# A macaron decoder layer with a two-part fp32 product: inputs moved by a few bytes in SBUF, the first three units and the first norm in finer pieces, four small loads moved apart

## What is computed

```python
for l in range(DEPTH):                                   # DEPTH = 1
    x = x + 0.5 * swiglu(rms_norm(x, norm_ffn1[l]), ffn1_gate[l], ffn1_up[l], ffn1_down[l])
    h = rms_norm(x, norm_mix[l])
    proj = h @ w_in[l]                                   # 1024 x 5120
    qa, ka, va, rb, kb, vb, ga, gb = jnp.split(proj, splits, axis=-1)
    y_a = moba_attention(to_heads(qa), to_heads(ka), to_heads(va), rel_bias)
    y_b = rwkv7_time_mix(h, rb, kb, vb, mix_rkv[l], mix_wag[l], w_lora_a[l], w_lora_b[l], ...)
    merged = jax.nn.sigmoid(ga) * (y_a @ proj_a[l]) + jax.nn.sigmoid(gb) * (y_b @ proj_b[l])
    x = x + merged @ w_out[l]
    x = x + 0.5 * swiglu(rms_norm(x, norm_ffn2[l]), ffn2_gate[l], ffn2_up[l], ffn2_down[l])
return rms_norm(x, norm_final)

def swiglu(h, w_gate, w_up, w_down):
    return (jax.nn.silu(h @ w_gate) * (h @ w_up)) @ w_down   # 1024 -> 2816 -> 1024
```

## Time and profile before

| | us |
|---|---|
| median of 3 runs | 646.39 |
| the profiled execution | 644.8 |
| its span (first to last instruction) | 643.0 |
| PE busy | 630.7 (98%), 6738 matmuls |
| PEld busy | 615.9 (96%) |
| DVE busy | 423.1 (66%) |
| ACT busy | 295.5 (46%) |
| DMA | 105.38 MB, 164 GB/s in the mean |

### The profile page before, as it was taken

One profiled execution on the slowest core, in us unless ns is written; L12 is line 12 of the kernel. 1 busy time (PEld: TensorE's weight loads), 2 busy tenths in 40 slices (PEclk: granted clock), 3 DMA queues, 4 the chain that ended last, 5 costly groups with the idle time before them and its releaser, 6 DMA issues.

```text
span 643.0 us, 15489 instructions
## 1 busy us (share of the span) xinstructions
PE 630.7 (98%) x6738; PEld 615.9 (96%) x6738; DVE 423.1 (66%) x491; ACT 295.5 (46%) x343; POOL 90.6 (14%) x91
## 2 busy tenths in 40 slices
PE   8899999999999999999999999999999999999996
PEld 8899999999999999999988999999999999999996
DVE  4766688665556369968994437877766566665662
ACT  5734554343434274334665544545543444443341
POOL 0026800000113000020005533006000000000120
PEclk9999999999999999999999999999999999999999
DMA  9667655555556335583332232355655566545541
GB/s 309 193 199 226 197 170 177 183 180 180 180 179 196 103 132 176 179 189 125 123 105 96 68 102 71 128 172 191 189 169 175 186 196 195 185 154 199 170 143 65
DMA packets 100608, 105.38 MB, mean 164 GB/s; under 512 B 2196, under 2 KB 98684, under 8 KB 100564
## 3 DMA queue, kind: packets, MB, share of 16 engines
q1 hardware_dynamic: 99348, 101.45, 48.9%
q0 software_dynamic: 1056, 3.02, 2.1%
q10 hardware_dynamic: 160, 0.27, 0.1%
HBM read 103.48 MB, written 1.25 MB: 163 GB/s over the span
## 4 chain that ended last, share of the span: by engine, by line
PE 88%; DVE 5%; DMA 3%; ACT 2%; issue 0%; SPq 0%; DVEq 0%; ACTq 0%
PE two L1426 26%; PE two L1428 24%; PE two L1427 24%; PE two L1422 10%; DVE w_lo L885 2%; DMA w_raw<-in_ffn_gate 1%; ACT w_hi L521 1%; DMA w_raw<-in_ffn_up 1%; DMA x_tok<-in_x 1%; PE two L1691 1%; DVE hlo_f L904 1%; PE two L1693 1%; PE two L1692 1%; PE two L1834 0%; DVE w_lo L895 0%
## 5 line engine op out<-in xcount | busy, mean ns | idle before, releaser
L521 ACT ACTIVATE w_hi<-w_raw 128x2048 fp32r<-128x2048 f32 (+1 forms) x87 | 164.2, 1887 | 257.7 <-PE two L1428 231.7
L885 DVE TENSOR_TENSOR w_lo<-w_raw,w_hi 128x2048 fp32r<-128x2048 f32 (+1 forms) x87 | 202.5, 2327 | 89.4 <-ACT w_hi L521 89.1
L1426 PE MATMUL two<-hlo_f,w_hi 128*128 128x256 f32 x656 | 185.0, 282 | 2.7 <-DVE w_lo L885 1.5
L1427 PE MATMUL two<-hhi_f,w_lo 128*128 128x256 f32 x656 | 184.6, 281 | 0.0
L1428 PE MATMUL two<-hhi_f,w_hi 128*128 128x256 f32 x656 | 184.6, 281 | 0.0
L1426 PEld LDWEIGHTS two<-hlo_f,w_hi 128*128 128x128 f32 x656 | 123.5, 188 | 4.1 <-DVE w_lo L885 2.1
L1427 PEld LDWEIGHTS two<-hhi_f,w_lo 128*128 128x128 f32 x656 | 123.5, 188 | 0.0
L1428 PEld LDWEIGHTS two<-hhi_f,w_hi 128*128 128x128 f32 x656 | 123.5, 188 | 0.0
L1426 PE MATMUL two<-hid_lo_t,w_hi 128*128 128x256 f32 x352 | 99.5, 283 | 0.0
L1427 PE MATMUL two<-hid_hi_t,w_lo 128*128 128x256 f32 x352 | 99.1, 281 | 0.0
L1428 PE MATMUL two<-hid_hi_t,w_hi 128*128 128x256 f32 x352 | 99.0, 281 | 0.0
(11 more groups left out here) (339 smaller groups left out, 962.5 us busy)
## 6 DMA issues: line engine op xcount, KB each, us to landing
w_raw<-in_ffn_up SPq DMA_DIRECT2D x22, 1024.0 KB, 5.4
w_raw<-in_ffn_gate SPq DMA_DIRECT2D x20, 1024.0 KB, 5.4
w_raw<-in_w_in SPq DMA_DIRECT2D x20, 1024.0 KB, 5.1
w_raw<-in_ffn_down SPq DMA_DIRECT2D x16, 896.0 KB, 4.6
w_raw<-in_ffn_down SPq DMA_DIRECT2D x8, 1024.0 KB, 5.0
w_raw<-in_w_out SPq DMA_DIRECT2D x4, 1024.0 KB, 5.0
w_raw<-in_proj_a SPq DMA_DIRECT2D x4, 512.0 KB, 3.5
w_raw<-in_proj_b SPq DMA_DIRECT2D x4, 512.0 KB, 4.1
```

The costliest lines, as they stand in the source:

```text
L521: nc.scalar.activation(whi[slot][:, 0:kts], raw[slot][:, 0:kts], ACT.Copy).then_inc(sg["hi_ready"], 1)
L885: nc.vector.tensor_tensor(wlo[slot][:, 0:kts], raw[slot][:, 0:kts], whi[slot][:, 0:kts].bitcast(F32), ALU.subtract).then_inc(sg["lo_ready" ...
L1426: mm(dst, whi[slot][:, k_, cols], xl, start=start, stop=False)
L1427: mm(dst, wlo[slot][:, k_, cols], xh, start=False, stop=False)
```

## The change

The diff has three parts.

First, the layout. The 32-byte tile `tok` leaves the top level (all later tiles of the mixing part move down by 32 bytes), and three unused tiles are put in: `pad_f` (192 bytes) before `hhi_f`, `pad_lora` (96) before `lora_whi`, `pad_y` (128) before `ybhi`. After that `hhi_f`, `hlo_f`, `hid_hi_t`, `hid_lo_t`, `hhi_m`, `hlo_m`, `yahi`, `yalo`, `ybhi`, `yblo`, `mhi`, `mlo` all have the remainder 32 against their weights, as has `hhi_m` against `lora_whi`; in the v units it is 224.

```diff
         idle = sb("idle", [P, 2])
-        tok = sb("tok", [P, 8])
...
             h_f = sb("h_f", [P, KD, T], scope=sc)
+            sb("pad_f", [P, 48], scope=sc)
             hhi_f = sb("hhi_f", [P, KD, T], F32R, scope=sc)
...
             rel = sb("rel", [NB, H], scope=sc)
+            tok = sb("tok", [P, 8], scope=sc)
...
             with ExitStack() as sc:
+                mb("pad_lora", [P, 24], scope=sc)
                 lora_whi = mb("lora_whi", [P, KD, 5 * P], F32R, scope=sc)
...
             with ExitStack() as sc:
+                mb("pad_y", [P, 32], scope=sc)
                 ybhi = mb("ybhi", [P, HT, T], F32R, scope=sc)
...
                 if f == 0:
-                    sp.dma_start(raw[0][:, 0:4], gate_w[0][:, 0:4, 0:W]).then_inc(w_landed[0], 16)
+                    sp.dma_start(raw[0][:, 0:2], gate_w[0][:, 0:2, 0:W]).then_inc(w_landed[0], 16)
+                    sp.dma_start(raw[0][:, 2:4], gate_w[0][:, 2:4, 0:W]).then_inc(sg["w0_mid"], 16)
                     sp.wait_ge(sg["x_in0"], 16)
...
                     sp.wait_ge(sg["x_in1"], 16)
-                    load(1, None, 1, up_w[0][:, :, 0:W])
+                    sp.dma_start(raw[1][:, 0:4], up_w[0][:, 0:4, 0:W]).then_inc(sg["w1_in"], 16)
                     sp.wait_ge(w_landed[0], 16)
+                    sp.dma_start(raw[1][:, 4:KD], up_w[0][:, 4:KD, 0:W]).then_inc(w_landed[1], 16)
                     sp.dma_start(raw2, gate_w[0][:, :, W:2 * W]).then_inc(w_landed[0], 16)
...
             nc.gpsimd.memset(lora_wlo[:, :, 4 * P + 64:5 * P].bitcast(F32), 0.0).then_inc(sg["pads_zero"], 1)
-            pool.wait_ge(sg["bias_row_sb"], 1)
-            pool.dma_start(bias_dram, bias_sb[:].unsqueeze(1).to_broadcast([H, 16, 384])).then_inc(sg["bias_out"], 16)
-
             pool.wait_ge(sg["multiplied"], 3)
...
                 pool.dma_start(s_g[:, ks_], lora_a[2][:, ks_]).then_inc(sg["lora_a_in"], 16)
+            pool.wait_ge(sg["multiplied"], 7)
+            pool.wait_ge(sg["bias_row_sb"], 1)
+            pool.dma_start(bias_dram, bias_sb[:].unsqueeze(1).to_broadcast([H, 16, 384])).then_inc(sg["bias_out"], 16)
             pool.wait_ge(sg["vec_ready"], 1)
...
-                if i % 2 == 0:
-                    act.wait_ge(sg["w0_in"] if n == 0 and i == 2 else w_landed[n], 16)
+                if n == 0 and i < 3:
+                    act.wait_ge((w_landed[0], sg["w0_mid"], sg["w0_in"])[i], 16)
+                elif n == 1 and i % 2 == 0:
+                    act.wait_ge(w_landed[1] if i else sg["w1_in"], 16)
                 ks_ = slice(2 * i, 2 * i + 2)
...
             for j in range(4):
-                first_hi(1, j)
                 act.wait_ge(sg[f"x_in{j // 2}"], 16)
...
                                      accum_out=tok[:, j:j + 1]).then_inc(sg["first_norm"], 1)
+                if j < 3:
+                    first_hi(1, j)
             act.wait_ge(sg["first_norm"], 5)
...
                                  scale=1.0 / D).then_inc(sg["rms_ready"], 1)
+            first_hi(1, 3)
...
-            def ffn(f, base, down):
+            def x_copy(j):
+                nc.vector.tensor_copy(x[:, 2 * j:2 * j + 2], bank[X_BANKS[j]][:].rearrange("p (c t) -> p c t", c=2))\
+                    .then_inc(sg["x_loaded"], 1)
+
+            def ffn(f, base, down, third_lo=None):
                 g0 = NG * f
...
-                body(0, nexts(0) if f else [lambda: None, nexts(0)[1]])
+                def copies_and_lo():
+                    for j in range(2, 4):
+                        x_copy(j)
+                    nexts(0)[1]()
+                    dve.wait_ge(sg["x_loaded"], 4)
+
+                body(0, nexts(0) if f else [third_lo, copies_and_lo])
                 if f == 0:
...
                 first_lo(0, j)
-            for j in range(4):
+            for j in range(3):
                 first_lo(1, j)
-                nc.vector.tensor_copy(x[:, 2 * j:2 * j + 2], bank[X_BANKS[j]][:].rearrange("p (c t) -> p c t", c=2))\
-                    .then_inc(sg["x_loaded"], 1)
+                if j < 2:
+                    x_copy(j)
             dve.wait_ge(sg["first_norm"], 4)
...
                                         ALU.mult, ALU.mult).then_inc(sg["first_norm"], 1)
+            first_lo(1, 3)
             dve.wait_ge(sg["first_hi"], 7)
...
                 .then_inc(sg["first_lo"], 1)
-            dve.wait_ge(sg["hi_ready"], 3)
-            nc.vector.tensor_tensor(wlo[0][:, 4:KD], raw2[:, 4:KD], whi[0][:, 4:KD].bitcast(F32), ALU.subtract)\
-                .then_inc(sg["lo_ready"], 1)
+
+            def third_lo():
+                dve.wait_ge(sg["hi_ready"], 3)
+                nc.vector.tensor_tensor(wlo[0][:, 4:KD], raw2[:, 4:KD], whi[0][:, 4:KD].bitcast(F32), ALU.subtract)\
+                    .then_inc(sg["lo_ready"], 1)
+
             dve.wait_ge(sg["first_norm"], 9)
-            dve.wait_ge(sg["x_loaded"], 4)
-            ffn(0, N_FFN1, N_DOWN1)
+            ffn(0, N_FFN1, N_DOWN1, third_lo)
             inverse_rms(1, slice(0, T + 2))
...
+                s = n % 2
                 for pair in range(4):
                     pe.wait_ge(sg["hlo_ready"], pair + 1)
-                    if pair == 3:
+                    if pair == (2 if n == 2 else 3):
                         pe.wait_ge(sg["lo_ready"], n + 1)
-                    else:
-                        pe.wait_ge(sg["first_lo"], 3 * n + pair + 1)
+                    elif pair < 3:
+                        pe.wait_ge(sg["first_lo"], 7 if n == 2 else 3 * n + pair + 1)
+                    if n == 2 and pair == 0:
+                        pe.wait_ge(sg["gate_taken"], 1)
                     if n == 1 and pair == 3:
...
                         for c in (2 * pair, 2 * pair + 1):
-                            dst, cols = bank[n][:, m * T:(m + 1) * T], slice(m * P, (m + 1) * P)
-                            part(dst, whi[n][:, c, cols], hlo_f[:, c], m + c == 0)
-                            part(dst, wlo[n][:, c, cols], hhi_f[:, c])
-                            last = part(dst, whi[n][:, c, cols], hhi_f[:, c])
+                            dst, cols = bank[s][:, m * T:(m + 1) * T], slice(m * P, (m + 1) * P)
+                            part(dst, whi[s][:, c, cols], hlo_f[:, c], m + c == 0)
+                            part(dst, wlo[s][:, c, cols], hhi_f[:, c])
+                            last = part(dst, whi[s][:, c, cols], hhi_f[:, c])
                 last.then_inc(sg["multiplied"], 1)
...
                     first_chunk(1)
-                    chunk(1, 0)
+                    first_chunk(2)
                     pe.wait_ge(sg["vec_in"], 16 * len(VECS))
...
             nc.tensor.transpose(bank[5][:, 0:KD], vec_rows[0:KD], ident[0:KD, 0:KD]).then_inc(sg["gain1_T"], 1)
-            warm(3)
+            warm(1)
             for q in range(4):
...
                 last.then_inc(sg["x_T"], 1)
-            warm(4)
+            warm(5)
             ffn(0, N_FFN1, N_DOWN1, 0)
```

More of the change, by code:

```diff
@@ L121 @@
 SIGNALS = """
-x_in0 x_in1 w0_in vec_in first_in const_in gain1_in gain1_T gain1_ready vecT x_T x_loaded vec_ready
+x_in0 x_in1 w0_mid w0_in w1_in vec_in first_in const_in gain1_in gain1_T gain1_ready vecT x_T x_loaded vec_ready
 hi_ready lo_ready multiplied
```

## The result

| | before | after |
|---|---|---|
| median of 4 runs each, us | 646.27 (645.88 to 647.35) | 637.26 (637.16 to 638.21) |
| ratio | | 0.9861, 95% interval 0.9844 to 0.9878 |
| the profiled execution, us | 644.8 | 637.18 |
| its span, us | 643.0 | 635.4 |

The change makes the kernel 9.0 us (7.9 to 10.1) faster. The forecast was 614.7 us with a range from 603 to 635: the sign was right, but the time lies above the range, and the gain is less than a third of the 31.7 us forecast.

A forecast was written before the change was run, and what follows sets the result against it. PE was taken to bound the kernel, by its matmul pitch and few stops. Layout 28.2, beginning 2.4 and lora loads 1.1 sum to 31.7 us: span 643.0 to 611.3, time 614.7 us, range 603 to 635.

The forecast's parts named there:

- What bounds the kernel: Whole kernel: PE is busy 630.7 of 643.0 us, so its pitch and the few places where it stops count.
- That the distance modulo 256 counts: Long products: pitch follows the input's distance to the weights modulo 256: 118.7 ns at 128, 117.7 at 64, 113.2 at 192.
- The pitch at 32: Long products after the layout: 111.6 ns per matmul at remainder 32, against a mean of 118.16 before.
- 4296 x (118.16 - p): Layout's gain over 4296 matmuls of the long products, p being the new pitch in ns: 28.2 us at 111.6.
- Rival 1: Long products: part of the interference stays at 32, p from 113.2 to 117.7, 628.0 us on the line; chance 0.20.
- the prediction's own sign: Whole kernel: the prediction is wrong in the main if the gain comes from the beginning and not the long stretches.
- Rival 3: Long products: no interference, PE's moving side binds at 109.2 ns, 42 us saved less some 0.6, 605 us; chance 0.25.
- The rule of the Trainium skill that loading weights steals nothing: PE's weight loads: by this rule the layout gives nothing, 642.9 us; the prediction held it as a rival, chance 0.05.
- The beginning: Units 0 to 3: unit 2 starts near 20.2, unit 3 at 28.0 instead of 30.37 behind a new wait; 2.4 us saved.
- The lora loads: PE's step at 60.03: spacing the bunched POOL loads by one unit each removes a late weight load's stall, 1.1 us.
- The ring: Weight slots' reload and split cycle: 9.8 us fit into two units of 10.7 at 111.6 ns, with 0.9 left.

The follow-up runs named there:

- The units on the idle chip: Kernels without the layer: only groups of 48 matmuls of the kernel's shape at chosen distances, other engines idle; 113.3 to 120.0 ns per matmul.
- The units with fewer columns: Bare groups of 48 matmuls, layer left out, with fewer weight or moving columns: 111.7 ns with 128 to 224 moving columns, never under 113.3 with 256.
- the version with 112: The changed kernel with its long products at distance 112 instead of 32, inputs shifted and weights left in place: 625.31 us, 0.9655 of the kernel before.

## Why the prediction was wrong, step by step

**What bounds the kernel** was right: PE's pitch, and a few stops.

**That the distance modulo 256 counts** was right as far as it went. The units on the idle chip reproduce 118.7, 117.8 and 113.3 at the distances of the kernel before, with a period of 256. It lacked two things: a place has a set of steady values and not one, and the weights' start modulo 32 is part of the place. The rows of the prediction show one value for each product, which I took for the value of its place. The same trace has both values at both places, in the products with `y` that the prediction did not read (first and 19th matmul of a stretch, `yahi` at remainder 64, then `ybhi` at 192):

```profile
411.51 0.28 PE L1428 MATMUL two<-yahi,w_hi 128*128 128x256 f32 x1
413.55 0.28 PE L1428 MATMUL two<-yahi,w_hi 128*128 128x256 f32 x1
414.25 0.28 PE L1428 MATMUL two<-ybhi,w_hi 128*128 128x256 f32 x1
416.37 0.28 PE L1428 MATMUL two<-ybhi,w_hi 128*128 128x256 f32 x1
```

2.04 / 18 = 113.3 ns at 64 and 2.12 / 18 = 117.8 at 192, the reverse of what `w_in` and `w_out` show. The sum had these 24 matmuls of `ybhi` at 113.4 with the rest.

**The pitch at 32** is the step that failed: 111.6 was forecast, and a gain of 3.9 us, if it is spread over the 4296 matmuls, means 118.16 - 0.9, about 117.2 in the mean. The term "4296 x (118.16 - p)" is 3.9 us by the stages and 3.1 by the layout alone, instead of 28.2. It failed in its bounds. The floor of 109 to 111.6 was read from matmuls with 128 moving columns or 2, and this shape has 256. The units with fewer columns show that up to 224 moving columns the load's 111.7 rules at any distance, and that with 256 nothing goes under 113.3. So the row of `silu` against itself, at remainder 0, said nothing of distance 0 for this shape: there the pitch is 120.0, the highest of the steady values in the table. And with 0 free and 64 slow, a step or a line between them was assumed for 32; the map has no such order.

**Rival 1** (p from 113.2 to 117.7, chance 0.20) is what happened, near its upper end of 641. Since the range was cut halfway to that end, the time fell outside it. By the prediction's own sign it was wrong in the main: of the 7.6 us between the two traces 3.7 come from the beginning and the lora loads. Rival 3 (109.2, chance 0.25) failed in the same bound as the forecast. Its formula, from the Trainium skill, "TensorE: Matmul & The Clock Gate", Part 2 (back-to-back issue gap), gives 109.2 ns for 256 columns; the Trainium skill calls this the isolated gap and has other figures there for a stream with a weight load before each matmul. No unit here with 256 moving columns goes under 113.3, so in these runs the measurement decides against it.

**The rule of the Trainium skill that loading weights steals nothing** ("TensorE: Matmul & The Clock Gate", Part 2, LDWEIGHTS) was rejected, and the runs partly agree with it: a part of what looked like stealing, from 109 to 113.3, is there with 4 weight columns as well. The rest is not as the rule says: at distance 0 the same 256 moving columns took 113.3 ns with 4 weight columns and 120.0 with 128.

**What got worse** was not priced. `w_out` was at 113.3 and went to 116.7 in its first unit and 117.8 in the others; the products with `ybhi` were at 113.3 in three quarters of their matmuls and went to 116.7. The sum had charged these 288 the common p and so a gain of 288 x 1.8 ns, 0.5 us, where the pitches mean a loss of about 1 us.

**The beginning** was right in place and size. Unit 2 at 20.71 (forecast 20.2), unit 3 at 27.56 (28.0), 2.8 us earlier where 2.4 were forecast. The new wait on unit 3's load is there, as ACT's 1.38 us. PE fills part of it with the transposes and the bias product. 0.4 us are given back up to unit 6, with a wait on `w_lo` at 39.31, before unit 5.

**The lora loads** were right: 1.1 forecast, 1.2 in the traces between units 6 and 8 (0.1 of it pitch), 2.1 (1.2 to 3.0) alone.

**The ring** was not tested at 111.6. At 113.3 it holds in FFN 1, where in the version with 112 no bracket stands before PE from 34 to 70 us, but not quite in the down products, where that version has the stop of 0.40 us shown above and four of 0.15 us, behind a wait of ACT for `w_raw`. The prediction's 0.9 us of room was worked out for units of 48 matmuls at a still shorter pitch; a down product has units of 42 between them, and no run here tells whether that is why.

## What to carry to other kernels

A bound must come from rows of the shape that it bounds: with half the moving columns the weight load was the limit, and it hid what the moving tile does. Before a value is taken for that of a place, look for a second stretch of the same place in the trace: the kernel before had one, with another value. Before laying out memory by a pattern read from four places, measure the map by itself; one small kernel of bare matmuls gave sixteen places in one run, and its best place gave 12 us more than the change. Where the same kernel's runs spread more than usual, compare one product's pitch between its stages: a steady value that changes only at interruptions means several patterns, and a place that has just one good one is worth more than a place whose best is as good.

## What the runs showed of the hardware

- With 128x128 float32r weights loaded before every 128x256 moving tile, the pitch at full clock takes steady values between 113.3 and 120.0 ns. They depend on the distance of the two starts modulo 256 bytes and on whether the weights start at a multiple of 32, and at seven of 16 places in the units also on the moment of entry. In the kernel before, remainder 64 showed both 113.3 and 117.8 as well.
- Once reached, a value held for as long as PE was not interrupted, through 21 units of FFN 2 (1008 matmuls) in the version with 112. There it was reached from the 13th matmul behind the entry on; in the units at distance 112 it took up to 15.
- With 128, 192 or 224 moving columns the pitch was 111.7 ns at all five distances tried.
- With 4 weight columns it was 113.3 or 116.7 ns for 256 moving columns: 116.7 always at distance 128, once in four at 64, never at 0, 112 and 192. Why there are two values even then, no run here tells; nor what in the memory makes the period of 256 bytes.
